# Output projection of a hybrid decoder step: token groups of 512, 512 and 32 instead of three of 352

## What is computed

```python
h = x + jnp.concatenate([o_g, o_d], axis=-1) @ w_out

hn = _rmsnorm(h, ffn_norm_g)
u, new_ffn = _causal_dwconv(hn @ w_up, ffn_buf, ffn_conv_w, ffn_conv_b)
y = h + (jax.nn.silu(u[..., :D_FF]) * u[..., D_FF:]) @ w_down
```

## Time and profile before

| | |
|---|---|
| median of three runs | 1811.03 us (1810.41 to 1812.68) |
| span of the profiled execution | 1812.4 us |
| TensorE busy | 1708.4 us, 94% |
| VectorE, ScalarE, GpSimd busy | 56%, 30%, 15% |
| mean granted TensorE clock over the span | 0.967 |
| output projection, first matmul to the first of the up projection | 925.0 to 1022.95 us |

### The profile page before, as it was taken

One profiled execution on the slowest core, in us unless ns is written; L12 is line 12 of the kernel. 1 busy time (PEld: TensorE's weight loads), 2 busy tenths in 40 slices (PEclk: granted clock), 3 DMA queues, 4 the chain that ended last, 5 costly groups with the idle time before them and its releaser, 6 DMA issues. The chain is left out here.

```text
span 1812.4 us, 28607 instructions
## 1 busy us (share of the span) xinstructions
PE 1708.4 (94%) x11114; PEld 1606.6 (89%) x11114; DVE 1006.6 (56%) x1480; ACT 541.6 (30%) x834; POOL 266.2 (15%) x446
## 2 busy tenths in 40 slices
PE   5999999997999999979779999999999999999998
PEld 4999999895888888846369999999999999999997
DVE  4544378774555555534544465565555656555654
ACT  4343342331343443443132231211221221221213
POOL 2100022124333333243200000000000000000000
PEclk9999999998899999986889999999999999999999
DMA  4311110321000110054341220110111111102103
GB/s 138 131 46 46 37 50 24 101 78 48 1 2 12 42 41 1 1 198 160 93 145 55 70 71 24 58 58 23 58 48 33 58 38 43 58 13 68 46 0 105
DMA packets 117239, 105.29 MB, mean 58 GB/s; under 512 B 6028, under 2 KB 104862, under 8 KB 115735
## 3 DMA queue, kind: packets, MB, share of 16 engines
q1 hardware_dynamic: 113586, 93.35, 16.9%
q0 software_dynamic: 2304, 8.39, 1.3%
q10 hardware_dynamic: 1270, 2.48, 0.4%
HBM read 86.13 MB, written 18.07 MB: 57 GB/s over the span
## 5 line engine op out<-in xcount | busy, mean ns | idle before, releaser
L2849 PE MATMUL f_up<-h_hi,w_hi 128*128 128x352 f32 x1032 | 335.1, 325 | 1.9 <-DVE w_lo L2638 1.2
L2849 PE MATMUL f_up<-h_hi,w_lo 128*128 128x352 f32 x1032 | 333.4, 323 | 0.0
L2849 PE MATMUL f_up<-h_lo,w_hi 128*128 128x352 f32 x1032 | 333.4, 323 | 0.0
L179 PE MATMUL proj<-x_hi,win_hi 128*128 128x352 f32 x672 | 226.3, 337 | 5.3 <-issue 3.0
L179 PE MATMUL proj<-x_hi,win_lo 128*128 128x352 f32 x672 | 216.6, 322 | 0.0
L179 PE MATMUL proj<-x_lo,win_hi 128*128 128x352 f32 x672 | 216.2, 322 | 0.0
L2849 PEld LDWEIGHTS f_up<-h_hi,w_hi 128*128 128x128 f32 x1032 | 193.8, 188 | 2.5 <-DVE w_lo L2638 1.5
L2849 PEld LDWEIGHTS f_up<-h_hi,w_lo 128*128 128x128 f32 x1032 | 194.1, 188 | 0.0
L2849 PEld LDWEIGHTS f_up<-h_lo,w_hi 128*128 128x128 f32 x1032 | 193.7, 188 | 0.0
L2856 PE MATMUL f_down<-f_g_hi,dn_hi 128*128 128x352 f32 x512 | 165.3, 323 | 0.0
L2856 PE MATMUL f_down<-f_g_hi,dn_lo 128*128 128x352 f32 x512 | 164.7, 322 | 0.0
(11 more groups left out here) (436 smaller groups left out, 3062.4 us busy)
## 6 DMA issues: line engine op xcount, KB each, us to landing
w_raw<-in_w_up SPq DMA_DIRECT2D x44, 512.0 KB, 3.8
win_raw<-in_w_in SPq DMA_DIRECT2D x28, 512.0 KB, 4.1
dn_raw<-in_w_down SPq DMA_DIRECT2D x11, 1024.0 KB, 5.1
p_key<-in_cache_k SPq DMA_DIRECT2D x32, 256.0 KB, 3.6
feat<-in_cache_v POOLq DMA_DIRECT2D x24, 256.0 KB, 4.7
x_scratch<-feat SPq DMA_DIRECT2D x1, 4224.0 KB, 13.3
feat<-x_scratch SPq DMA_DIRECT2D x8, 528.0 KB, 8.4
feat<-in_x_prompt SPq DMA_DIRECT2D x8, 512.0 KB, 8.1
```

Source lines behind the costliest of these rows:

```text
L179: mm = nc.tensor.matmul(out, w[:, k, :], x[:, k, g * TG:(g + 1) * TG], start=(k == 0 and i == 0), stop=(k == KT - 1 and i == 2))
L2849: mm = nc.tensor.matmul(up[u % RING][:, 0:TG], a[s][:, kk, :], b, start=(kk + x == 0), stop=(kk == KT - 1 and x == 2))
```

## The change

A list `OUT` gives the three groups of the output projection: tokens 0 to 511, 512 to 1023 and 1024 to 1055, the last being the 32 sample tokens. The residual adds, the matmuls of tile 0 and those of tiles 1 to 7 use it. The call of `project_group` is replaced by the same loops written out. The input projection, the MLP and its `TG` stay as they are.

```diff
+    OUT = [slice(0, 512), slice(512, SEQ), slice(SEQ, T)]
...
-                h = hT[:, n, g * TG:(g + 1) * TG]
-                nc.vector.tensor_tensor(h, up[u % RING][:, 0:TG], h, ALU.add).then_inc(unit_kept, 1)
+                h = hT[:, n, OUT[g]]
+                nc.vector.tensor_tensor(h, up[u % RING][:, 0:OUT[g].stop - OUT[g].start], h, ALU.add).then_inc(unit_kept, 1)
...
-                    at = slice(g * TG, (g + 1) * TG)
+                    at = OUT[g]
                     for x, (a, b) in enumerate(((w_hi, o_hi), (w_hi, o_lo), (w_lo, o_hi))):
-                        mm = nc.tensor.matmul(up[g][:, 0:TG], a[0][:, k, :], b[:, k, at], start=(k + x == 0), stop=(k == KT - 1 and x == 2))
+                        mm = nc.tensor.matmul(up[g][:, 0:at.stop - at.start], a[0][:, k, :], b[:, k, at], start=(k + x == 0), stop=(k == KT - 1 and x == 2))
...
-                    project_group(nc, up[u % RING][:, 0:TG], g, w_hi[s], w_lo[s], o_hi, o_lo).then_inc(unit_done, 1)
+                    at = OUT[g]
+                    for k in range(KT):
+                        for x, (a, b) in enumerate(((w_hi, o_hi), (w_hi, o_lo), (w_lo, o_hi))):
+                            mm = nc.tensor.matmul(up[u % RING][:, 0:at.stop - at.start], a[s][:, k, :], b[:, k, at],
+                                                  start=(k + x == 0), stop=(k == KT - 1 and x == 2))
+                    mm.then_inc(unit_done, 1)
```

## The result

| | before | after |
|---|---|---|
| median | 1811.86 us (4 runs, 1810.41 to 1813.26) | 1833.94 us (4 runs, 1833.05 to 1836.38) |
| ratio | | 1.0126, 95% interval 1.0112 to 1.0140 |
| span of the profiled execution | 1812.4 us | 1834.8 us |
| output projection, first matmul to the first of the up projection | 97.96 us | 119.94 us (925.25 to 1045.19) |

The kernel became 22.1 us slower, and the profiled spans differ by 22.4 us. All but 0.4 us of that is in the output projection. The page after names the same engine for the chain as the earlier trace rows. The shares of that line add to about half of the span, since the chain is followed back only to the start of the output projection, in both kernels; in that half it is almost all TensorE.

The account below looks back on a forecast made before the run. The prediction took TensorE to bound the kernel: 17.9 us for wide and narrow matmuls plus 4.3 us for clock falls made +22.2 us, added with the difference between span and median to give 1833.2 us, range 1826 to 1839.

Parts of the forecast that it names:

- What bounds the kernel: Whole kernel: the chain that ended last is almost all TensorE, so a microsecond added to its stream lengthens the kernel equally.
- The 32-column matmul, 112 ns: Output projection: each narrow matmul waits for its own weight load, 112 ns from start to start, 13 if loads were hidden.
- The 512-column matmul, 229 ns between 225 and 231: Output projection: a wide matmul costs 225 ns with 12 ns paid per matmul, 231 if proportional to columns; 229 taken.
- 192 x 93 = 17.9 us: Output projection: 192 triples of matmuls each grow from 477 to 570 ns, 93 ns more, adding 17.9 us.
- VectorE and the hand-over at nothing: Residual adds and start of the up projection: no new wait for TensorE, costed at nothing; under 1 us if wrong.
- The clock, 2.5 x 1.7 = 4.3 us: Output projection: narrow runs make the clock fall 2 to 3 times, 3.4 us at half pace, each losing 1.7 us.
- (a): Rival, output projection: the clock holds and only the loads count, +12.5 to +18.6 us, best 1828.9; chance 0.22.
- (b): Rival, output projection: the clock falls after nearly every narrow run or stays low, +29.8 us and above, 1841; chance 0.11.
- (c): Rival, output projection: a narrow matmul costs only an issue floor, its load running ahead; +1.7 to +8.6 us; chance 0.05.
- (d): Rival, output projection: faster, narrow loads hidden and wide matmuls free of the 12 ns; -6.5 us, 1804.5; chance 0.02.

Follow-up runs that it names:

- cut32: The changed kernel with the output projection's 32-column matmuls loading only the first 32 of their 128 weight columns; 1817.16 us, ratio 1.0034.
- turn_mid: The changed kernel with the turning of the small rows behind the first 512-column group of tiles 1 to 4, not the 32-column group; 1842.20 us, ratio 1.0171.
- narrow_twice: The changed kernel with the 24 matmuls of the 32-column group run twice in tiles 1 to 7; 1870.08 us, ratio 1.0316.
- the interleaved kernel: The changed kernel with 32-column matmuls one by one between the second group's 512-column ones in tiles 1 to 7; 1832.76 us, then 1830.90 us.

## Why the prediction was right

The forecast was 1833 us in a range of 1826 to 1839, and 1833.9 was measured, by the mechanism named. Step by step:

- **What bounds the kernel.** Right for the part that counts, though the earlier trace rows shows a chain that covers only 49% of the span and says nothing of the time ahead of the output projection. 21.98 of the 22.4 us between the profiled spans lie in the output projection.
- **The 32-column matmul, 112 ns.** Right and shown: 24 in 2.59 us, and 0.03 us apart once the load was a quarter (cut32). The one that waits is shifted by a place: the first narrow one of a run is free, and the wide one behind the run pays.
- **The 512-column matmul, 229 ns between 225 and 231.** It came out at the upper end: (11.21 - 0.09) / 48 = 232 ns, where the 0.09 are the load exposed behind the narrow run. The 12 ns beside the columns go with the columns and are not paid once for each matmul: 118 ns at 256 columns, 159 at 352, 232 at 512. A triple costs 13.80 us / 24 = 575 ns instead of the 570 of the sum.
- **192 x 93 = 17.9 us.** From the starts of the tiles in both profiles, tiles 1 to 4 took 50.06 us before and 60.32 after, tiles 5 to 7 34.47 and 43.00, with one fall of 1.56 us in each group. At full clock the seven grew by 15.67 us; with 8 x 3 x 98 ns = 2.35 for tile 0 that is 18.0 us. With the 575 ns alone it would be 192 x 98 = 18.8 us: a tile with a turning behind it grew by 2.17 us and one without by 2.32, in part because the 0.15 us wait for a DMA was gone. So the sum was met by two small errors against each other.
- **VectorE and the hand-over at nothing.** Right; no new wait.
- **The clock, 2.5 x 1.7 = 4.3 us.** The mechanism was right, and its size was built of two wrong parts. A tile's wide run with a fall in it took 12.78 us instead of 11.22, so a fall costs 1.56 us and not 1.7. At half clock 512 columns take 427 ns, which is 512 / 1.2 and less than twice 232. There were two falls in the first profile and three in the second, 3.1 and 4.7 us. The places, behind tiles 1 to 4, held in all five; the reason I gave for them, that the turning has to follow, did not (turn_mid).
- **What the sum left out.** The start of the stretch ran 6.1 us at half clock instead of 3.8, which is about 0.8 us more: tile 0 grew by 3.2 us, of which 2.35 are loads and widths. 18.0 + 3.1 + 0.8 = 21.9 us against 21.98 found in the profile and 22.2 forecast. That the forecast came so near is in part luck: it gave the falls 1.2 us too much and left out the 0.8 us at the start. Why the half clock lasts longer there in one execution than in another was not settled: the changed kernel reached 1.00 after 6.1 us in its first profile and after 2.9 us in its second.
- **The rivals.** (a) is refuted for runs of this kind by narrow_twice, yet what it gives, a loss by loads alone, is what the interleaved kernel shows: 117.7 us. (b) would have needed longer runs, as in narrow_twice. (c) and (d) fall by the 0.11 us between starts, and the Trainium skill's gap rule for few columns ("TensorE: Matmul & The Clock Gate", section "Back-to-back issue gap"), by which the kernel would hardly have moved, does not hold here: 24 narrow ones took 2.59 us, 108 ns each, and not 25. Only the second of each run is recorded 0.03 us behind the first, and it lasts 0.26 us against 0.18, waiting for its load. The nearest to 25 ns in a stream are cut32's 32 ns with a quarter of the load; whether the load or some floor sets those 32 was not tried. The section itself warns that small ones are undercounted for want of the load.

## What to carry to other kernels

Where each matmul loads its own 128 weight columns, a matmul with fewer than about 250 fp32r data columns costs as much as one with 250 (112 ns here): divide a dimension that does not fit one bank into parts that all have that many, equal (352) or not (400, 400, 256), and not into full banks and a rest. If a narrow rest can't be avoided, put its matmuls between wide ones; it costs the same loads, but in two profiles the clock was spared (3.4 us by the medians, with intervals that overlap). Look at the granted clock behind every run of load-bound matmuls, even where TensorE shows no idle time.

## What the runs showed of the hardware that I had not expected

- A narrow matmul exposes a load even when wide ones stand on both sides, 340 ns for a pair of 512 and 32 columns against 232 + 13 for their columns. It is as if one load ran ahead and not two.
- At full clock fp32r data columns take about 0.453 ns each (232 ns for 512, 182 for 400), 9% over 1 / 2.4 GHz; at half clock they take exactly 1 / 1.2 GHz (427 ns for 512). What the 9% are was not tried.
- A run of 24 matmuls in 2.6 us, with weight loads back to back and no idle time, can be followed by 3.4 us at half clock; with 160 data columns in place of 32, at the same pace of loads, no fall came in the seven runs of the one profile.
